# The opening of a two-layer trunk in another order: weight unit behind two rows, first projection by steps, forget-gate sum in the third

## The chip, the cores and the metric

The kernel runs on one core of a Trainium2 chip. The metric is device microseconds (us) for one execution. All times of the trace are counted from the start of the profiled span.

## The reference, cut to what matters

The trunk has two layers on 512 tokens of 1024 channels. Layer 0 mixes tokens by forgetting attention with 16 heads of 64 channels; layer 1 by a gated recurrence. After each mixer follow a layer norm, a gated ConvFFN (2816 wide), a second layer norm and a gated embedding. The change touches the start of layer 0 alone:

```python
proj = x @ w_in
q, k, v, fg = jnp.split(proj, [D_MODEL, 2 * D_MODEL, 3 * D_MODEL], axis=-1)
log_f = jax.nn.log_sigmoid((fg + b_f).astype(jnp.float32))
c = jnp.cumsum(log_f, axis=1).transpose(0, 2, 1)
logits = jnp.einsum("bhqd,bhkd->bhqk", q_i, k).astype(jnp.float32) * scale
logits = logits + c_i[..., None] - c[:, :, None, :]
probs = jax.nn.softmax(logits, axis=-1)
```

## The kernel before, in words

**Storage.** Activations lie channels first: eight tiles of 128 channels by 512 tokens (`x[:, m, :]`, "rows" below). Every float32 product is made of three products of a high and a low part (`three`, L402): high by high (L404), weight high by input low (L405), weight low by input high (L406). ScalarE (ACT) makes the high part of an input row (L1186), VectorE (DVE) the low part (L913). Weights come in units of 512 KB, eight 128x128 blocks, which the SP queue loads into one of four stage slots (L333) and GpSimd (POOL) splits, one instruction for the high part (L386) and four for the low part (L390), after a tiny instruction (L384) that waits for the load and for the last user of the slot.

**Order of the opening.** Each engine's order is written out by hand; semaphores join them.

- SP issues the loads of rows 0 to 3 (L303, two rows each), then weight units (L333). ACT issues the forget gate's weights `wf` and bias `bf` (L1178, L1179), rows 4 to 7 (L1181) and the column constants (L1182).
- TensorE (PE) first multiplies all eight rows by the forget weights, plain float32 of two passes a row (L447), once both `wf` and `bf` are there. Then it waits for all eight low parts (L556) and makes the projections of head pair 0: q to bank 0, k to bank 1, v to bank 0 (`project`, L472, over `whole_tile`, L408, 24 matmuls each). Between the eight steps of a projection other work is hung in (`beside`): the transposes of the forget gate (`turn_forget`, L455) in the first; the cumulative sum (`sum_forget`, L463) and blocks 0 to 2 of the turn of x to tokens (`first_block`, L440) in the second; the turn of columns (`turn_columns`, L553) and blocks 3 to 7 in the third. `sum_forget` waits for DVE's log-sigmoid steps (L921 to L928, some 16 small instructions, with one exponential on ACT, L1190).
- DVE then prepares the lambda of the recurrence (L934, L936), reads the queries (L944 to L953), copies the cumulated rows (L995, L997), makes the low part of the keys (`keys_low`, L960), and finishes the lambda chain (`log1p_twice`, L840 to L853, L1003 to L1007) before the first softmax maxima (L968).
- ACT copies the first three turned blocks (L1176), stores the cumulated rows to DRAM (L1194), waits for that store, loads a pair's rows back and reads the keys out of bank 1 (`keys`, L1205 and L1210), then copies `flat` (L1265) and the other five blocks, and the values (L1218).
- The first scores (L485 to L489) wait for the turned blocks, queries, low keys and rows. From there a loop over head pairs interleaves the projections of pair j with scores, turned probabilities (L505) and value sums (L517) of pair j - 1.

Of the kernel before, what the change touches and what calls it, by code (L numbers as in the profile page):

```python
# [21 lines left out]
P = 128  # L22
SEQ = 512
D_MODEL = 1024
DEPTH = 2
# [8 lines left out]
KT = D_MODEL // P  # L34
# [98 lines left out]
def hybrid_trunk_kernel(nc, xT, pT, w_square, w_down, w_forget, b_forget, w_lru, columns, outT):  # L133
    phases = plan()
    with ExitStack() as ctx:
        def sem(name):
            return ctx.enter_context(nc.semaphore(name))
# [18 lines left out]
        x = place("x", [P, KT, SEQ], F32)  # L156
# [22 lines left out]
        a = [tmp_at]  # L179
# [4 lines left out]
        a = [shared]  # L184
# [48 lines left out]
        unit_split = sem("unit_split")  # L233
        unit_used = sem("unit_used")
        x_loaded = [sem(f"x_loaded{n}") for n in range(KT // 2)]
        fg_w_loaded, cols_loaded = sem("fg_w_loaded"), sem("cols_loaded")
        consts_set = sem("consts_set")
        x_hi_ready, x_lo_ready = sem("x_hi_ready"), sem("x_lo_ready")
        mix_hi_ready, mix_lo_ready = sem("mix_hi_ready"), sem("mix_lo_ready")
# [59 lines left out]

        @block.sync  # L300
        def _(sp):
            for n in range(KT // 4):
                sp.dma_start(x[:, 2 * n:2 * n + 2, :], xT[:, 2 * n:2 * n + 2, :]).then_inc(x_loaded[n], 16)  # L303
            def norm_rows(n):
                if n == 0:
                    sp.wait_ge(flat_stored, 16)
                else:
                    sp.wait_ge(norm_ready, n * 2 * QT)
                src = rows_dram[n // 2, (n % 2) * 16:(n % 2) * 16 + 16, :].rearrange("a n -> (a n)")
                sp.dma_start(rows[:].rearrange("p a n -> p (a n)"),  # L310
                             src.partition_broadcast(P)).then_inc(rows_loaded, 16)

            square_first = 0
            for name, ph in phases.items():
                base, n, layer = square_first, len(ph.slots), int(name[-1]) if name[-1] in "01" else 0
                for i in rounds(sp, ph):
                    for r, place_at in enumerate(ph.slots):
                        s = place_at % SLOTS
                        sp.wait_ge(unit_split, ph.stage_free(i, r))
                        to = stage[:, s, :]  # L320
                        if name.startswith("down") or name.startswith("out"):
                            half, kp = r // (n // 2), r % (n // 2)
                            w, u = (w_down, layer * KT + half * 4) if name.startswith("down") else \
                                (w_square, base + half * 4)
                            src = w[u:u + 4, :, kp * 2 * P:(kp + 1) * 2 * P].rearrange("a p n -> p a n")
                            to = to.rearrange("p (a n) -> p a n", a=4)
                        elif name in ("rgx", "rgg"):
                            src = w_square[base + (r // 2) * 4 + r % 2 + (2 if name == "rgg" else 0)]
                        elif ph.iters == 1:
                            src = w_square[base + r]  # L330
                        else:
                            src = w_square[bass.ds(i * n + (base + r), 1), :, :].rearrange("a p n -> (a p) n")
                        sp.dma_start(to, src).then_inc(unit_loaded[s], 16)  # L333
                if name == "qkv":
                    norm_rows(0)
                if name.startswith("up"):
                    norm_rows(2 * layer + 1)
                if name == "gate0":
                    norm_rows(2)
                    sp.wait_ge(unit_used, phases["down0"].done(0, FT - 1))  # L340
                    sp.dma_start(w_ai[:], w_lru.rearrange("m p n -> p m n")).then_inc(lru_w_loaded, 16)
                if name == "rgg":
                    square_first += 2 * n
                elif name != "rgx" and not name.startswith("down"):
                    square_first += ph.iters * n

            for m in range(KT):
                sp.wait_ge(emb_added, KT + m + 1)
                sp.dma_start(outT[m], x[:, m, :]).then_inc(stored, 16)
            sp.wait_ge(stored, 16 * KT)  # L350
# [45 lines left out]
        def _(pe):  # L396
# [43 lines left out]
                    mm = pe.transpose(banks[bank][:, t * P:(t + 1) * P], x[:, m, t * P:(t + 1) * P], ident[:])  # L440
                mm.then_inc(block_turned, 1)

            pe.wait_ge(fg_w_loaded, 32)
            for k in range(KT):
                if k % 2 == 0:
                    pe.wait_ge(x_loaded[k // 2], 16)
                mm = pe.matmul(banks[5][0:HEADS, :], wf[:, k, :], x[:, k, :], start=(k == 0), stop=(k == KT - 1))  # L447
            mm.then_inc(fg_done, 1)

            def turn_forget():  # L450

# [20 lines left out]
            def project(j, r, bank, beside={}):  # L472
                whole_tile(qkv, j, r, bank, in_hi, in_lo, beside)
# [67 lines left out]
            def first_block(m):  # L541

                if m >= 3:
                    pe.wait_ge(x_tok_ready, m - 2)
                turn_block(m, 2 + m % 3)

            def turn_columns():
# [3 lines left out]
                for layer in range(DEPTH):  # L551
# [1 line left out]
                    mm = pe.transpose(banks[6][0:32, P + layer * P:2 * P + layer * P], cols[:, c:c + 32], ident[:])  # L553
                mm.then_inc(flat_done, 1)

            pe.wait_ge(x_lo_ready, KT)  # L556
            project(0, 0, 0, {1: turn_forget})
            project(0, 1, 1, {3: sum_forget, 4: lambda: first_block(0), 5: lambda: first_block(1),
                              6: lambda: first_block(2)})
            pe.wait_ge(q_read, 1)  # L560
            project(0, 2, 0, {1: turn_columns, 2: lambda: first_block(3), 3: lambda: first_block(4),
                              4: lambda: first_block(5), 5: lambda: first_block(6), 6: lambda: first_block(7)})
            pe.wait_ge(x_tok_ready, KT)
            pe.wait_ge(flat_read, 1)
            with pe.Fori(1, PAIRS) as j:
# [271 lines left out]
        def _(dve):  # L837
# [76 lines left out]
                                  ALU.subtract).then_inc(x_lo_ready, 1)  # L914


            dve.wait_ge(fg_done, 1)
            dve.tensor_scalar(z_chan[:], banks[5][0:HEADS, :], bf[:, 0:1], None, ALU.add).then_inc(fg_chan, 1)
            z, e, r0, r1, acc, minus_log = (fg[:, n, :] for n in range(6))
# [240 lines left out]
        def _(act):  # L1160
# [13 lines left out]
            def token_block(m, bank):  # L1174
                act.wait_ge(block_turned, m + 1)
                act.copy(x[:, m % KT, :], banks[bank][:]).then_inc(x_tok_ready, 1)  # L1176

            act.dma_start(wf[:], w_forget).then_inc(fg_w_loaded, 16)  # L1178
            act.dma_start(bf[:], b_forget).then_inc(fg_w_loaded, 16)  # L1179
            for n in range(KT // 4, KT // 2):  # L1180
                act.dma_start(x[:, 2 * n:2 * n + 2, :], xT[:, 2 * n:2 * n + 2, :]).then_inc(x_loaded[n], 16)  # L1181
            act.dma_start(cols[:], columns).then_inc(cols_loaded, 16)  # L1182
# [5 lines left out]

            act.wait_ge(fg_abs, 1)
            act.activation(fg[:, 1, :], fg[:, 1, :], ACT.Exp, scale=-1.0).then_inc(fg_exp, 1)  # L1190
            for m in range(3):
                token_block(m, 2 + m % 3)
            act.wait_ge(fg_rows, 1)
            act.dma_start(c_dram, c_rows[:].bitcast(F32)).then_inc(fg_stored, 16)  # L1194
# [19 lines left out]
            def values(j, turned):  # L1214
                act.wait_ge(unit_used, phases["qkv"].done(j, 2))
                if turned:
                    act.wait_ge(vt_done, j)
                act.copy(v_chan[:], banks[0][:]).then_inc(kv_read, 1)  # L1218

            def token_values(j):  # L1220
                act.wait_ge(vt_done, j + 1)
# [39 lines left out]
            act.sem_inc(pt_read, 1)  # L1261
            act.sem_inc(exp_ready, 1)
            keys(0, False)
            act.wait_ge(flat_done, 1)
            act.copy(flat[:].rearrange("p a n -> p (a n)"), banks[6][0:32, P:P + DEPTH * P]).then_inc(flat_read, 1)  # L1265
            for m in range(3, KT):
                token_block(m, 2 + m % 3)
            act.wait_ge(flat_read, 1)
            act.dma_start(rows_dram.rearrange("l r n -> r l n"), flat[:]).then_inc(flat_stored, 16)
            values(0, False)  # L1270
# [222 lines left out]
```

## Time and profile before

| what | value |
|---|---|
| median of 3 runs | 1329.36 us (1327.84 to 1331.38) |
| the profiled execution | 1330.12 us |
| its span | 1328.4 us |
| PE busy | 1297.2 us, 98% |
| granted TensorE clock, mean | 0.993 |
| POOL, DVE, ACT busy | 858.2, 539.0, 407.7 us |
| HBM traffic | 117.83 MB read, 2.20 MB written |

The profiled execution is 0.76 us longer than the median. Its span covers first to last instruction; 1.7 us lie around it. A timeline row gives start, duration, engine, line, operation, tiles and, in brackets, the idle time before it with what ended it. PE starts are exact, but matmul durations overlap the next one; start-to-start distances are used. A granted clock of 1.00 is the 2.4 GHz level, 0.50 the 1.2 GHz level.

### The profile page before, as it was taken

To read this page: it belongs to the slowest core of one execution; us is meant where nothing else is said; L and a number is where in the kernel's file an instruction comes from. 1 tells how busy PE (TensorE), PEld (TensorE's weight loads), DVE (VectorE), ACT (ScalarE), POOL (GpSimd) and SP (SyncE) were. 2 spreads that over 40 slices of the span, in tenths; PEclk is the share of its full clock that TensorE was granted. 3 is DMA by queue.
4 is the path that set the end of the run, shared out by engine and by line. 5 is a ranking of instruction groups with operands and counts; after the bars stand their busy time and mean duration, and the time that the engine had idled before them with its cause. 6 is when DMAs were issued, how large, how long until landed. Compare 5 with 4: busy or idle time off the path is not lost.

```text
span 1328.4 us, 17615 instructions
## 1 busy us (share of the span) xinstructions
PE 1297.2 (98%) x5758; PEld 1018.8 (77%) x5758; DVE 539.0 (41%) x826; ACT 407.7 (31%) x678; POOL 858.2 (65%) x1166
## 2 busy tenths in 40 slices
PE   6999999998999999999999999998999999999998
PEld 3766666676888888888888767877888888888886
DVE  6533344445444444411073357173444444301252
ACT  1443343411433333300033367112333333300041
POOL 6343445524978787777767645737877778777563
PEclk9999999998999999999999999998999999999999
DMA  5111113211232223333324222312322233333221
GB/s 183 52 48 63 48 51 108 80 47 64 96 107 97 95 95 126 95 111 95 99 90 161 79 80 64 109 47 83 111 95 95 97 99 130 111 101 95 80 88 55
DMA packets 57146, 120.58 MB, mean 91 GB/s; under 512 B 3744, under 2 KB 35808, under 8 KB 56592
## 3 DMA queue, kind: packets, MB, share of 16 engines
q1 hardware_dynamic: 56048, 117.45, 27.0%
q10 hardware_dynamic: 1056, 2.58, 0.6%
q8 instruction: 25, 0.41, 0.1%
q14 instruction: 17, 0.14, 0.0%
HBM read 117.83 MB, written 2.20 MB: 90 GB/s over the span
## 4 chain that ended last, share of the span: by engine, by line
PE 81%; issue 6%; ACT 3%; POOL 3%; DVE 2%; POOLq 2%; ACTq 1%; DMA 1%; DVEq 0%; SPq 0%
PE bank L404 17%; PE bank L406 16%; PE bank L405 16%; PE bank L424 6%; PE bank L423 6%; PE bank L425 6%; PE bank L517 3%; PE bank L655 2%; PE bank L656 2%; PE bank L660 2%; POOLq L387 2%; ACT probs L1232 1%; POOL w_lo L390 1%; POOL far_lo L390 1%; POOLq L385 1%
## 5 line engine op out<-in xcount | busy, mean ns | idle before, releaser
L390 POOL TENSOR_TENSOR w_lo<-stage,w_hi 128x256 fp32r<-128x256 f32 x800 | 589.5, 767 | 29.4 <-issue 0.3
L386 POOL TENSOR_SCALAR w_hi<-stage 128x1024 fp32r<-128x1024 f32 x200 | 210.5, 1053 | 179.1 <-PE bank L425 74.6
L404 PE MATMUL bank<-x_hi,w_hi 128*128 128x512 f32 x704 | 274.4, 390 | 0.0
L406 PE MATMUL bank<-x_hi,w_lo 128*128 128x512 f32 x704 | 274.0, 389 | 0.0
L405 PE MATMUL bank<-x_lo,w_hi 128*128 128x512 f32 x704 | 274.0, 389 | 0.0
L384 POOL TENSOR_TENSOR waiter<-waiter 128x1 f32<-128x1 f32 x112 | 24.8, 221 | 238.2 <-PE bank L406 161.5
L406 PEld LDWEIGHTS bank<-x_hi,w_lo 128*128 128x128 f32 x704 | 132.2, 188 | 27.4
L405 PEld LDWEIGHTS bank<-x_lo,w_hi 128*128 128x128 f32 x704 | 132.2, 188 | 27.3
L404 PEld LDWEIGHTS bank<-x_hi,w_hi 128*128 128x128 f32 x704 | 132.2, 188 | 27.3
L1034 DVE SCALAR_TENSOR_TENSOR tmp<-bank,cols,tmp 128x511 f32<-128x511 f32 x88 | 65.9, 749 | 207.7 <-ACT tmp L1288 196.7
L404 PE MATMUL bank<-in_hi,w_hi 128*128 128x512 f32 x320 | 138.7, 433 | 1.9 <-POOL w_lo L390 1.4
L424 PE MATMUL bank<-w_lo,h_hi 128*128 128x512 f32 x352 | 138.7, 394 | 0.0
L423 PE MATMUL bank<-w_hi,h_hi 128*128 128x512 f32 x352 | 138.4, 393 | 0.0
L425 PE MATMUL bank<-w_hi,h_lo 128*128 128x512 f32 x352 | 136.7, 388 | 0.0
L405 PE MATMUL bank<-in_lo,w_hi 128*128 128x512 f32 x320 | 126.6, 396 | 0.0
L406 PE MATMUL bank<-in_hi,w_lo 128*128 128x512 f32 x320 | 126.4, 395 | 0.0
L863 DVE SCALAR_TENSOR_TENSOR bank<-x,bank 128x512 f32<-128x512 f32 x32 | 22.2, 693 | 204.3 <-PE bank L425 203.4
L1288 ACT ACTIVATE tmp<-bank,cols 128x512 f32<-128x512 f32 x88 | 63.8, 776 | 60.0 <-PE bank L406 59.7
L404 PEld LDWEIGHTS bank<-in_hi,w_hi 128*128 128x128 f32 x320 | 60.5, 189 | 25.7 <-issue 16.0
L423 PEld LDWEIGHTS bank<-w_hi,h_hi 128*128 128x128 f32 x352 | 66.1, 188 | 15.2
L425 PEld LDWEIGHTS bank<-w_hi,h_lo 128*128 128x128 f32 x352 | 66.1, 188 | 14.8
L424 PEld LDWEIGHTS bank<-w_lo,h_hi 128*128 128x128 f32 x352 | 66.2, 188 | 13.0
(166 smaller groups left out, 1763.1 us busy)
## 6 DMA issues: line engine op xcount, KB each, us to landing
stage<-w_square SPq DMA_DIRECT2D x164, 512.0 KB, 3.3
stage<-w_down SPq DMA_DIRECT2D x44, 512.0 KB, 3.7
rows<-norm_rows SPq DMA_DIRECT2D x4, 1024.0 KB, 5.6
outT<-x SPq DMA_DIRECT2D x8, 256.0 KB, 2.0
x<-xT SPq DMA_DIRECT2D x2, 512.0 KB, 5.1
x<-xT ACTq DMA_DIRECT2D x2, 512.0 KB, 8.4
p_in<-pT ACTq DMA_DIRECT2D x2, 512.0 KB, 3.3
w_ai<-w_lru SPq DMA_DIRECT2D x1, 1024.0 KB, 8.4
```

The costliest lines, as they stand in the source:

```text
L386: pool.tensor_scalar(high[:, s, :], stage[:, s, :], 1.0, 0.0, ALU.mult, ALU.add)
L387: pool.drain()
L390: piece = pool.tensor_tensor(low[:, s, to], stage[:, s, to], high[:, s, to].bitcast(F32), ALU.subtract)
L404: pe.matmul(out, w_hi[:, s, c:c + P], m_hi, start=first, stop=False)
L405: pe.matmul(out, w_hi[:, s, c:c + P], m_lo, start=False, stop=False)
L406: return pe.matmul(out, w_lo[:, s, c:c + P], m_hi, start=False, stop=last)
L423: pe.matmul(four(out), m_hi, wide_hi, start=first, stop=False)
L424: pe.matmul(four(out), m_hi, wide_lo, start=False, stop=False)
L425: return pe.matmul(four(out), m_lo, wide_hi, start=False, stop=last)
L517: mm = pe.matmul(banks[7][h * HEAD_DIM:(h + 1) * HEAD_DIM, kt * P:SEQ], v_tok[:, kt, h * HEAD_DIM:(h + 1) * HEAD_DIM], probs_t[:, c0:c0 + ...
L1034: dve.scalar_tensor_tensor(t[:, 1:SEQ], banks[r][:, 0:SEQ - 1], cols[:, bass.ds(c + 1, 1)], t[:, 1:SEQ], ALU.mult, ALU.add)
L1288: act.activation(tmp[:, r, :], banks[r][:], ACT.Identity, bias=cols[:, bass.ds(c + 3, 1)], scale=cols[:, bass.ds(c + 2, 1)]).then_inc(conv ...
```

## The change

SP loads only rows 0 and 1 and goes on to the weight units; rows 2 and 3 go to ACT's queue, behind `wf` and ahead of `bf`, and `bf` has a semaphore of its own that DVE waits for. PE multiplies rows 0 to 5 by the forget weights, waits for weight unit 0, and then runs the q projection step by step, each step waiting for its own low part alone; the forget products of rows 6 and 7 stand ahead of its steps 0 and 1, the forget transposes ahead of step 6. The k projection has four turned blocks, the v projection the forget sum (ahead of its step 1), the columns and four blocks, and it writes to bank 5, so that the wait for the queries' read goes. ACT copies `flat` and all eight turned blocks before it stores the cumulated rows and takes up the keys.

```diff
-            for n in range(KT // 4):
-                sp.dma_start(x[:, 2 * n:2 * n + 2, :], xT[:, 2 * n:2 * n + 2, :]).then_inc(x_loaded[n], 16)
+            sp.dma_start(x[:, 0:2, :], xT[:, 0:2, :]).then_inc(x_loaded[0], 16)
...
-            pe.wait_ge(fg_w_loaded, 32)
-            for k in range(KT):
+            def forget(k):
                 if k % 2 == 0:
                     pe.wait_ge(x_loaded[k // 2], 16)
                 mm = pe.matmul(banks[5][0:HEADS, :], wf[:, k, :], x[:, k, :], start=(k == 0), stop=(k == KT - 1))
-            mm.then_inc(fg_done, 1)
+                if k == KT - 1:
+                    mm.then_inc(fg_done, 1)
...
-            pe.wait_ge(x_lo_ready, KT)
-            project(0, 0, 0, {1: turn_forget})
-            project(0, 1, 1, {3: sum_forget, 4: lambda: first_block(0), 5: lambda: first_block(1),
-                              6: lambda: first_block(2)})
-            pe.wait_ge(q_read, 1)
-            project(0, 2, 0, {1: turn_columns, 2: lambda: first_block(3), 3: lambda: first_block(4),
-                              4: lambda: first_block(5), 5: lambda: first_block(6), 6: lambda: first_block(7)})
+            pe.wait_ge(fg_w_loaded, 16)
+            for k in range(KT - 2):
+                forget(k)
+            unit_ready(qkv, 0, 0)
+            for k in range(KT):
+                if k < 2:
+                    forget(KT - 2 + k)
+                pe.wait_ge(x_lo_ready, k + 1)
+                if k == KT - 2:
+                    turn_forget()
+                mm = three(banks[0][:], 0, k * P, in_hi[:, k, :], in_lo[:, k, :], k == 0, k == KT - 1)
+            mm.then_inc(unit_used, 1)
+            project(0, 1, 1, {1: lambda: first_block(0), 3: lambda: first_block(1), 5: lambda: first_block(2),
+                              6: lambda: first_block(3)})
+            project(0, 2, 5, {0: sum_forget, 1: turn_columns, 2: lambda: first_block(4), 3: lambda: first_block(5),
+                              4: lambda: first_block(6), 5: lambda: first_block(7)})
...
+            dve.wait_ge(fg_b_loaded, 16)
             dve.wait_ge(fg_done, 1)
...
             act.dma_start(wf[:], w_forget).then_inc(fg_w_loaded, 16)
-            act.dma_start(bf[:], b_forget).then_inc(fg_w_loaded, 16)
+            act.dma_start(x[:, 2:4, :], xT[:, 2:4, :]).then_inc(x_loaded[1], 16)
+            act.dma_start(bf[:], b_forget).then_inc(fg_b_loaded, 16)
...
-            for m in range(3):
+            for m in range(4):
+                token_block(m, 2 + m % 3)
+            act.wait_ge(flat_done, 1)
+            act.copy(flat[:].rearrange("p a n -> p (a n)"), banks[6][0:32, P:P + DEPTH * P]).then_inc(flat_read, 1)
+            for m in range(4, KT):
                 token_block(m, 2 + m % 3)
             act.wait_ge(fg_rows, 1)
...
-                act.copy(v_chan[:], banks[0][:]).then_inc(kv_read, 1)
+                act.copy(v_chan[:], banks[0 if turned else 5][:]).then_inc(kv_read, 1)
...
             keys(0, False)
-            act.wait_ge(flat_done, 1)
-            act.copy(flat[:].rearrange("p a n -> p (a n)"), banks[6][0:32, P:P + DEPTH * P]).then_inc(flat_read, 1)
-            for m in range(3, KT):
-                token_block(m, 2 + m % 3)
             act.wait_ge(flat_read, 1)
```

## Rows read from the trace of the kernel before

**Rows 1.** Chain that ended last, 0 to 62 us: start, us, what

```profile
35.94 1.93 DMA forget_rows<-c_rows
...
41.03 0.69 DVE k_b L960
...
49.41 0.70 DVE stat L968
```

**Rows 2.** Timeline of ACT: high parts of the rows, and what they waited for

```profile
5.51 1.14 ACT L1186 CAST in_hi<-x 128x512 fp32r<-128x512 f32 x2 [0.61 <-DMA x<-xT]
6.81 1.14 ACT L1186 CAST in_hi<-x 128x512 fp32r<-128x512 f32 x2 [0.15 <-DMA x<-xT]
9.07 1.14 ACT L1186 CAST in_hi<-x 128x512 fp32r<-128x512 f32 x2 [1.13 <-DMA x<-xT]
11.63 1.14 ACT L1186 CAST in_hi<-x 128x512 fp32r<-128x512 f32 x2 [1.42 <-DMA x<-xT]
```

**Rows 3.** DMA queues in 5 to 6 us: packets, MB, share (q1 SP, q10 ACT)

```profile
q1 hardware_dynamic: 88, 0.30, 74.5%
q10 hardware_dynamic: 39, 0.11, 27.7%
```

**Rows 4.** DMA queues in 9 to 10 us

```profile
DMA packets 106, 0.42 MB, mean 422 GB/s; under 512 B 3, under 2 KB 3, under 8 KB 106
```

**Rows 5.** Timeline of POOL: splits of units 0, 1 and 5

```profile
9.89 0.58 POOL L384 TENSOR_TENSOR waiter<-waiter 128x1 f32<-128x1 f32 x1 [5.71 <-DMA stage<-w_square]
...
17.24 2.81 POOL L390 TENSOR_TENSOR w_lo<-stage,w_hi 128x256 fp32r<-128x256 f32 x4
...
46.27 2.81 POOL L390 TENSOR_TENSOR w_lo<-stage,w_hi 128x256 fp32r<-128x256 f32 x4
```

**Rows 6.** The forget products (L447) alone in two stretches: PE busy (x instructions)

```profile
6.03:9.16 3.13, 3.13 (x4) 0.58 (x5) 1.00 1.02 408
9.16:14.47 5.31, 5.31 (x13) 1.07 (x11) 1.00 0.69 275
```

**Rows 7.** Timeline of PE

```profile
6.03 8.44 PE L447 MATMUL bank<-x,wf 128*16 128x512 f32 x16 [6.03 <-DMA bf<-b_forget]
15.88 0.47 PE L404 MATMUL bank<-in_hi,w_hi 128*128 128x512 f32 x1 [1.41 <-POOL w_lo L390]
...
22.11 0.39 PE L404 MATMUL bank<-in_hi,w_hi 128*128 128x512 f32 x1
...
28.34 3.47 PE L463 MATMUL bank<-up_to,fg 128*16 128x512 f32 x8 [3.28 <-DVE fg L928]
...
33.01 0.60 PE L440 MATMUL bank<-ident,x 128*128 128x128 f32 x4
...
34.16 0.60 PE L440 MATMUL bank<-ident,x 128*128 128x128 f32 x4
...
43.32 0.60 PE L440 MATMUL bank<-ident,x 128*128 128x128 f32 x4
...
45.00 0.49 PE L485 MATMUL bank<-k_a,q_a 66*128 66x512 f32 x1 [0.38 <-issue]
...
52.98 0.50 PE L485 MATMUL bank<-k_a,q_a 66*128 66x512 f32 x1
...
60.28 0.55 PE L505 MATMUL bank<-ident,probs 128*128 128x128 f32 x3 [1.03 <-ACT probs_t L1242]
```

**Rows 8.** Timeline of DVE

```profile
17.91 0.23 DVE L921 COPY fg<-bank 128x64 f32<-128x64 f32 x1 [2.65 <-PE bank L455]
...
47.10 0.62 DVE L853 SCALAR_TENSOR_TENSOR lam<-lam 128x8 f32<-128x8 f32 x1
```

**Rows 9.** Line 851 alone, 15 to 60 us: ns min/median/max, first and last start

```profile
L851 DVE SCALAR_TENSOR_TENSOR lam<-lam x7: 166/168/959, 44.2 to 46.5; 128x8 f32<-128x8 f32 x7
```

**Rows 10.** Stretches by clock: PE, PEld, DVE, ACT, POOL busy, PEclk, DMA share, GB/s

```profile
29.37:32.78 3.41, 3.41 (x10) 1.44 (x8) 3.19 (x5) 0.00 (x0) 0.00 (x0) 0.50 0.44 154
316.09:322.92 6.83, 5.63 (x17) 3.94 (x15) 1.48 (x3) 0.00 (x0) 6.47 (x10) 0.50 0.36 136
```

More of the change, by code:

```diff
@@ L235, in hybrid_trunk_kernel @@
         x_loaded = [sem(f"x_loaded{n}") for n in range(KT // 2)]
-        fg_w_loaded, cols_loaded = sem("fg_w_loaded"), sem("cols_loaded")
+        fg_w_loaded, fg_b_loaded, cols_loaded = sem("fg_w_loaded"), sem("fg_b_loaded"), sem("cols_loaded")
         consts_set = sem("consts_set")
```

## The prediction

> **What bounds the kernel now.** I read the page first: PE is busy 98% of the span, so a change of order can only win or lose where PE stands or runs slowly. PE's timeline shows where it stands in the opening: until 6.03 us, for `bf`; 1.41 us before 15.88, for the split of unit 0; 3.28 us before 28.34, for the forget steps; 0.38 us before 45.00; 1.03 us before 60.28, for ACT [rows 7]. The stretches by clock add one thing: after that stand of 3.28 us the granted clock is 0.50, the 1.2 GHz level, from 29.37 to 32.78 [rows 10]. But a PE gap only counts if the chain that ended last runs through it. That chain goes, in the opening, over unit 0, the forget steps, the forget sum (28.34), three turned blocks that follow, the store of the cumulated rows (35.94), the low keys (41.03), the lambda chain on DVE, the first maxima (49.41), and ACT's exponentials, and it comes back to PE at 60.28 [rows 1, 7]. PE itself is off it from 36 to 60 us. So two chains have to be carried through to 60.28: one over PE, one over ACT and DVE. From there on PE is nearly always busy, and a shift stays.
>
> **The parts, worked out.** The sum is made against the profiled execution.
>
> *Loads.* SP's queue brought rows 0, 1 at 5.51 and rows 2, 3 at 6.81, ACT's queue rows 4, 5 at 9.07 and rows 6, 7 at 11.63 [rows 2]; unit 0 came at about 9.8, when POOL began [rows 5]. Each is 0.52 MB. Now unit 0 stands where rows 2, 3 stood, so I take 6.8. Rows 2, 3 take the place of rows 4, 5 (9.1), rows 4, 5 that of rows 6, 7 (11.6), and rows 6, 7 come after. All queues together move 0.42 MB a us [rows 4]; 0.5 MB more, with SP's queue running dry midway, gives 13.2 (bounds: 1.3 us behind 11.6, the full rate, which is 12.9; 2.6 us, the half, 14.2). A load moved to ACT's queue thus comes 2.3 us later, because that queue had only 0.11 of 0.41 MB in 5 to 6 us [rows 3]. The Trainium skill, "DMA: Bandwidth & Descriptors", "Queues, rings and completion order", says that each DMA engine takes turns between the queues it has work for; were the shares even from the start, rows 2, 3 would be there by about 7.2 and rows 6, 7 by 12.0, PE would be free for unit 0 at 12.5, and the sum below would be 0.9 us better. The row decides here: the shares were uneven.
>
> *Forget products.* Without `bf` PE starts at 5.55, not 6.03. A pass costs 3.13/4 = 0.8 us at first and 0.43 later [rows 6]. Rows 0, 1: four passes, to 8.95. Rows 2, 3 from 9.1 to 10.8; rows 4, 5 from 11.6 to 13.35. Unit 0 is no wait: POOL starts at 6.9 and needs 5.9 at most (9.89 to 15.74), 4.3 at the pace of unit 1 (ready at 20.05) [rows 5], so it is split by 11.2 to 12.8. PE begins the q projection at 13.4, where it began at 15.88 [rows 7].
>
> *First projection.* 15.88 to 22.11 is 6.2 us [rows 7], with the forget transposes in it; the four forget passes moved in add 1.75. End: 21.35, against 22.11. That is only 0.75 earlier: the early start is mostly spent on the forget products that were there anyhow. The waits for single low parts are nothing: the last low part is there by about 15.5 (13.2, 1.14 for ACT's two [rows 2], then DVE's) and step 7 comes at 20.7. `bf`'s wait on DVE is for a load that lands before fg_done (about 16).
>
> *Second projection.* 24 matmuls are 5.6, a turned block adds 0.45 (33.01 to 34.16 is a block and three matmuls, 1.15 [rows 7]): 7.4, to 28.75. ACT copies these blocks as they come; it has nothing else.
>
> *Forget sum.* The transposes end at 19.9 now (17.9 before [rows 8]), two us later. The DVE steps took 17.9 to 28.3, 10.4 us, since most ran beside POOL's splits: with POOL busy a small DVE step costs 0.62 [rows 8], with POOL idle 0.17 [rows 9]. POOL's fourth split waits for PE's last use of unit 0 (21.35) and ends 4.3 later, at about 25.7, and seven steps of 0.3 behind it give 27.8; were they slow to the end, 30.3. PE comes to the sum at 28.75 + 0.7 = 29.45. I take no stand; the bound is 0.85. The sum, 3.47 us with the clock mostly at 0.50 [rows 7, 10], is 2.15 at 1.00 by the widths 512, 384, 256, 128. So the third projection has its step 1 at 31.6.
>
> *Third projection.* Three steps with the columns (0.15) and three blocks come before the eighth block: 4 x 0.7 + 0.7 + 0.15 + 3 x 0.45 = 5.0. The eighth block is turned at 36.6, against 43.32 [rows 7], and the projection ends at 38.45. With bank 5 there is no wait for the queries; it would have bound nothing here before either. The cumulated rows (DVE, two copies after the queries) are ready at about 33.9 and wait for ACT.
>
> *Keys.* Here the change gives back. ACT stores the cumulated rows behind the eighth block, not the third. From the start of the copy before the store (35.9) to the low keys (41.03) is 5.1 us [rows 1]. Copy at 36.6 + 0.65 = 37.25, low keys at 42.35, against 41.03: 1.3 later. They take 1.5, so the first scores start at 43.85, against 45.00 [rows 7]. PE has stood 5.4 us by then. A stand of 3.28 us was followed by 3.41 us at half clock, which cost 1.7; another stretch had 6.83 us, 3.4 [rows 10]. I take the nearer, 1.7; bounds 0 and 3.4.
>
> *The two chains to 60.28.* PE: 43.85, plus 7.85 to the second scores (45.00 to 52.98 less a short wait), plus 1.7, is 53.4, against 52.98; plus 6.1 to the transposes (7.3 less 1.03 of stand) is 59.5. DVE: low keys to maxima took 8.4 [rows 1]. Seven of its steps ran beside POOL's split that starts with the third projection's end (46.27 is its low part [rows 5]) at 0.6 or more. Now that split runs 38.6 to 43, before the lambda chain, so seven steps cost 0.24 instead of 0.6 on average: 4.23 becomes 1.7, the chain 5.8. Maxima at 48.15 (49.41 before), which does not bind PE. The second head's maxima follow PE's scores: 53.4 + 1.9, plus 4.2 to PE's need, is 59.5 again. So 59.5 against 60.28: **0.8 us saved**, 1329.3 for the profiled execution (1330.12), and as that lies 0.76 above the median, 1328.6 on the median's scale.
>
> **What a measurement can tell.** 0.3% is 4.0 us, so 1325.4 and 1333.4 are the borders. The working has no 4 us in either direction.
>
> **Rivals.**
> - *A, slower: keys behind the token copies, and a cold PE.* Place: ACT's queue before the store. If rows 6, 7 come at 14.2 (+1.0), the forget steps stay slow (+0.85), and the half clock lasts 6.83 us (3.4), PE is back at 59.5 + 1.0 + 0.85 + 1.7 = 63.05: 2.8 slower, 1332.2. It decides from an eighth block at 37.4 on (with 1.7 for the clock). Beyond 4 us it would need that block after 39.7. For it: the bounds above. Against: PE's work up to there is counted in rows. Chance 0.20, of which 0.09 is past 4.0.
> - *B: the lambda chain stays slow.* 8.4 us put the maxima at 50.75, the second scores at 54.3, and PE back at 60.4 to 61.4: about 0.1 to 1.1 slower, 1330. The row against it is the 0.17 [rows 9]. A rule speaks against it too: the Trainium skill, "SBUF — State Buffer", "Who interferes with whom", has VectorE instructions with two SBUF inputs and GpSimd ones that read SBUF block each other wholly; 0.17 and 0.62 for such steps agree. Chance 0.15.
> - *C, faster: the clock is spared.* No half clock after the stand: 57.8 against 60.28, 2.5 saved, 1326.9. If, besides, one of the later half-clock stretches such as 316.09 to 322.92 (3.4 us [rows 10]) fell away with the new timing, it would be 5.9, 1323.5. Chance 0.15, of which 0.08 is past 4.0.
> - *D: the order does nothing*, because the first projection still ends near 22. It does end at 21.35, but the forget stand of 3.28 us goes anyway, by its later place; if all that were lost again before 60.28, it would be 1329.4. Chance 0.05.
> - The forecast itself: 0.45.
>
> **The numbers.** Predicted 1328.6. The range takes C without the later stretch and A up to its price, with 1 us for the runs' own spread: 1325.2 to 1332.8. Faster by over 0.3% has 0.08, slower 0.09, within 0.83.
>
> **What would show it.** Right: q projection near 13.4; no PE stand at 25 to 28; forget sum in some 2.2 us; eighth block near 36.6; a PE stand of 5 us before scores at 43.9, then half clock; low keys near 42.4; lambda steps all near 0.17; third transposes (60.28) near 59.5. Wrong: rows 6, 7 later than 14.2, an ACT queue that takes up the keys later than 40, or a second stand of over 1 us between 44 and 60.

## The result and the profile after

The changed kernel takes 1332.3 us (median of 19 runs, 1330.66 to 1334.65) against 1330.1 us of the kernel before (19 runs beside them). The ratio is 1.0020, with a 95% interval of 1.0014 to 1.0027: slower by 2.7 us (the medians differ by 2.2), less than the 0.3% that was set as a border, but clear of the noise, and not the 0.8 us gain of the forecast. The forecast of 1328.6 was counted from the median of three runs, 1329.36.

The profiled execution spans 1331.8 us, 3.4 more than before. It took 1333.66 us, 1.4 above the median, while the profile of the kernel before lies on its median. Eight of the 19 executions had a mean granted clock of 0.990, as the profiled one, and ten had 0.992. The marks below thus show one of the slower executions, with a stretch of half clock that others probably lack; run a3 shows what that is worth. In what follows a "stand" is a time in which PE waits between two instructions, and "half clock" a granted clock of 0.50.

The chain that ended last, kernel after, 0 to 66 us (start, us, what), is the place to begin:

```profile
1.56 7.06 DMA stage<-w_square
...
13.43 1.18 POOL w_lo L389
14.65 1.03 PE bank L446 x2
...
17.24 1.82 PE bank L446 x2
...
40.29 0.45 PE bank L439 x4
40.77 1.94 DMA forget_rows<-c_rows
...
45.86 0.68 DVE k_b L970
...
47.53 0.79 PE bank L485
...
59.85 0.70 DVE stat L978
...
63.77 0.59 ACT probs_t L1257
64.40 0.55 PE bank L505 x3
```

It runs over unit 0, then over PE up to the eighth turned block, and from there over ACT's store of the cumulated rows (L1209) and the low keys to the first scores. The lambda chain, which stood in it before [rows 1], is gone from it. In its place stands PE itself, from 47.53 on.

PE's timeline, kernel after, has the same marks as [rows 7]:

```profile
5.66 6.89 PE L446 MATMUL bank<-x,wf 128*16 128x512 f32 x12 [5.66 <-DMA wf<-w_forget]
14.65 1.03 PE L446 MATMUL bank<-x,wf 128*16 128x512 f32 x2 [2.11 <-POOL w_lo L389]
...
24.56 0.40 PE L403 MATMUL bank<-in_hi,w_hi 128*128 128x512 f32 x1
...
32.71 2.33 PE L463 MATMUL bank<-up_to,fg 128*16 128x512 f32 x8
...
40.13 0.60 PE L439 MATMUL bank<-ident,x 128*128 128x128 f32 x4
...
47.53 0.79 PE L485 MATMUL bank<-k_a,q_a 66*128 66x512 f32 x1 [5.40 <-DVEq L972]
...
57.98 0.39 PE L485 MATMUL bank<-k_a,q_a 66*128 66x512 f32 x1
...
64.40 0.55 PE L505 MATMUL bank<-ident,probs 128*128 128x128 f32 x3 [0.27 <-ACT probs_t L1257]
```

| mark on PE | before | forecast | after |
|---|---|---|---|
| first projection begins | 15.88 | 13.4 | 14.65 |
| second projection begins | 22.11 | 21.35 | 24.56 |
| forget sum | 28.34 | 29.45 | 32.71 |
| eighth block turned | 43.32 | 36.6 | 40.13 |
| first scores | 45.00 | 43.85 | 47.53 |
| second scores | 52.98 | 53.4 | 57.98 |
| third transposes of the first head ("the return") | 60.28 | 59.5 | 64.40 |

The return is the mark by which the experiments are compared below; in the changed kernel it is 4.1 us late. The span is only 3.4 us longer, for 0.7 came back later: PE's last stand of the layer norm is 0.87 us where it was 1.20, and one near 790 us is 0.67 where it was 1.06.

Two stretches of the changed kernel are at half clock (columns as in [rows 10]):

```profile
15.67:19.08 3.41, 3.41 (x7) 0.97 (x6) 0.00 (x0) 0.00 (x0) 3.26 (x5) 0.50 0.44 154
46.39:53.22 6.83, 5.69 (x18) 4.29 (x19) 5.12 (x22) 1.25 (x3) 0.13 (x1) 0.50 0.23 83
```

The first follows a stand of 2.11 us, the second begins in one of 5.40. The kernel before had one stretch of 3.41 us, after 3.28 us of stand.

ACT's and POOL's timelines, kernel after, show when rows and unit 0 came and how long the split took:

```profile
5.71 2.18 ACT L1197 CAST in_hi<-x 128x512 fp32r<-128x512 f32 x4
10.10 1.14 ACT L1197 CAST in_hi<-x 128x512 fp32r<-128x512 f32 x2 [2.21 <-DMA x<-xT]
12.68 1.14 ACT L1197 CAST in_hi<-x 128x512 fp32r<-128x512 f32 x2 [1.43 <-DMA x<-xT]
```

```profile
8.87 0.19 POOL L383 TENSOR_TENSOR waiter<-waiter 128x1 f32<-128x1 f32 x1 [4.70 <-DMA stage<-w_square]
...
10.44 4.17 POOL L389 TENSOR_TENSOR w_lo<-stage,w_hi 128x256 fp32r<-128x256 f32 x4
14.56 0.64 POOL L383 TENSOR_TENSOR waiter<-waiter 128x1 f32<-128x1 f32 x1
```

Rows 2 and 3 were there by 6.8 (ACT goes through four rows without a wait), rows 4 and 5 at 10.1, rows 6 and 7 at 12.7: all earlier than forecast. Unit 0 came at 8.7, later than forecast, and its low part took 4.17 us where unit 1's took 2.81 [rows 5]. Unit 0 was slow before the change too (POOL timeline, kernel before):

```profile
12.07 3.67 POOL L390 TENSOR_TENSOR w_lo<-stage,w_hi 128x256 fp32r<-128x256 f32 x4
```

### The profile page after: what moved, and what is told of

It is laid out like the page before. It is cut to its first block, busy times and chain, and to the rows that moved or that the text cites. A ratio compares the mean times of both kernels' runs of the same rounds, so it can differ in the third digit from the quotient of the medians.

```text
span 1331.8 us, 17615 instructions
## 1 busy us (share of the span) xinstructions
PE 1300.0 (98%) x5758; PEld 1019.8 (77%) x5758; DVE 532.3 (40%) x826; ACT 407.9 (31%) x678; POOL 858.5 (64%) x1166
## 4 chain that ended last, share of the span: by engine, by line
PE 83%; issue 5%; ACT 3%; POOL 3%; POOLq 2%; DVE 1%; ACTq 1%; DMA 1%; DVEq 0%; SPq 0%
PE bank L403 17%; PE bank L405 17%; PE bank L404 17%; PE bank L423 6%; PE bank L422 6%; PE bank L424 6%; PE bank L517 3%; PE bank L664 2%; PE bank L665 2%; PE bank L669 2%; POOLq L386 1%; ACT probs L1247 1%; POOL w_lo L389 1%; POOL far_lo L389 1%; PE bank L485 1%
```

## The experiments

Each kernel is compared with runs of the kernel before on the same chip. "Return" is the mark of the table above, from one profiled execution (60.28 before, 64.40 after). The ratios rest on 10 to 12 executions of each kernel, b7's on 5 and c1's on 6, and for the change itself on 19.

| run | ratio to before | 95% interval | first scores | return |
|---|---|---|---|---|
| the change | 1.0020 | 1.0014 to 1.0027 | 47.53 | 64.40 |
| a1 first part alone | 1.0018 | 1.0008 to 1.0027 | 46.93 | 62.53 |
| a2 second part alone | 1.0012 | 1.0003 to 1.0021 | 45.31 | 62.12 |
| a3 early keys | 1.0013 | 1.0004 to 1.0022 | 44.38 | 61.78 |
| a4 products before scores | 1.0004 | 0.9995 to 1.0013 | 47.56 | 62.36 |
| b5 forget products ahead | 1.0005 | 0.9996 to 1.0014 | 45.07 | 62.15 |
| b6 products at both stands | 0.9997 | 0.9988 to 1.0006 | 46.60 | 61.40 |
| b7 all mended | 0.9963 | 0.9949 to 0.9976 | 42.82 | 58.67 |
| b8 loads back | 1.0022 | 1.0013 to 1.0032 | 48.94 | 65.39 |
| c1 mended, 18 products | 0.9970 | 0.9958 to 0.9982 | 43.03 | 57.33 |
| c2 mended, none | 0.9992 | 0.9983 to 1.0001 | 42.75 | 59.44 |
| c3 before, lambda moved | 0.9987 | 0.9979 to 0.9996 | 45.03 | 59.02 |
| c4 mended, loads back | 0.9975 | 0.9967 to 0.9984 | 43.61 | 57.60 |

**a1: the first part alone.** Loads, forget products and first projection as changed; the rest, ACT's order and v's bank included, as before.

```diff
-            project(0, 1, 1, {1: lambda: first_block(0), 3: lambda: first_block(1), 5: lambda: first_block(2),
-                              6: lambda: first_block(3)})
-            project(0, 2, 5, {0: sum_forget, 1: turn_columns, 2: lambda: first_block(4), ...
+            project(0, 1, 1, {3: sum_forget, 4: lambda: first_block(0), 5: lambda: first_block(1),
+                              6: lambda: first_block(2)})
+            pe.wait_ge(q_read, 1)
+            project(0, 2, 0, {1: turn_columns, 2: lambda: first_block(3), ...
```

> The kernel before with the first part alone: the loads, the forget products and the first projection by steps as changed; second and third projections, banks and ACT's order as before. Theory 1 (in the changed kernel a late unit 0 and the half-clock stretch behind PE's 2.1 us stand push the end of the first projection from 22.1 to 24.5, and the way of the keys adds the rest): the forget steps end near 31, the forget sum starts 2.7 us later than before, everything up to the transposes at 60.28 shifts by it, 1332.8 or 2.7 us slower than before. Theory 2 (the first part is neutral, ACT's late keys alone cost the time): within 0.7 us of before.

The time is near the expected 2.7 us (2.4 by the ratio) and speaks against theory 2, but it does not come by the expected steps. PE timeline of a1, and a row of its stretches by clock:

```profile
14.15 1.03 PE L446 MATMUL bank<-x,wf 128*16 128x512 f32 x2 [0.81 <-POOL w_lo L389]
...
29.56 4.45 PE L463 MATMUL bank<-up_to,fg 128*16 128x512 f32 x8 [4.10 <-DVE fg L939]
```

```profile
27.53:34.36 6.83, 4.80 (x9) 1.43 (x10) 5.58 (x14) 0.00 (x0) 0.42 (x1) 0.50 0.24 77
```

Here the stand before the unit was 0.81 us and no half clock followed, and still the forget sum is 1.2 us late and takes 4.45 us instead of 3.47. The first part, with its forget transposes ahead of step 6, feeds DVE's forget steps later; in the old second projection that makes a stand of 4.10 us where there were 3.28, and 6.83 us of half clock around it where there were 3.41. The scores are 1.9 us late and the return 2.25.

**a2: the second part alone.** Projections 2 and 3, bank 5 and ACT's order as changed; loads and first projection as before.

```diff
-            project(0, 1, 1, {3: sum_forget, 4: lambda: first_block(0), ...
-            pe.wait_ge(q_read, 1)
-            project(0, 2, 0, {1: turn_columns, 2: lambda: first_block(3), ...
+            project(0, 1, 1, {1: lambda: first_block(0), 3: lambda: first_block(1), ...
+            project(0, 2, 5, {0: sum_forget, 1: turn_columns, 2: lambda: first_block(4), ...
```

> The kernel before with the rest of the change alone: forget sum in the third projection with its own bank, four turned blocks in the second, ACT's keys behind all turned blocks; loads, forget products and first projection as before. Theory 1 (both parts cost, each by a clock stretch): eighth block turned at 37.4, low keys at 43.1, first scores at 44.7, a half-clock stretch behind the stand, PE back at the transposes at 60.5 to 62.2 instead of 60.28: 0.2 to 1.9 us slower than before. Theory 2 (late keys alone are the cause): as slow as the whole change, 2.2 us or more.

Theory 1 holds. The scores start after the same stand of 5.40 us as in the changed kernel, with 6.82 us of half clock around them; a row of stretches and one of PE's timeline of a2:

```profile
44.73:51.55 6.82, 6.24 (x19) 4.74 (x20) 4.73 (x21) 1.24 (x3) 0.00 (x0) 0.50 0.23 78
```

```profile
45.31 0.79 PE L485 MATMUL bank<-k_a,q_a 66*128 66x512 f32 x1 [5.40 <-DVEq L961]
```

The return is 1.84 us late. The two losses add up to 4.09, against 4.12 for the whole change, but that is luck: a1 loses by a stand before the forget sum, which the whole change does not have, and the whole change by half clock before 20 us, which a1 does not have. Each part does cost something without the other. Theory 2 of this run, 2.2 us or more, is unlikely by the return; the ratio alone (0.4 to 2.8 us) does not exclude it.

**a3: keys behind the fifth block.**

```diff
-            for m in range(4, KT):
-                token_block(m, 2 + m % 3)
+            token_block(4, 2 + 4 % 3)
             act.wait_ge(fg_rows, 1)
...
             keys(0, False)
+            for m in range(5, KT):
+                token_block(m, 2 + m % 3)
```

> The changed kernel, but ACT stores the cumulated rows and reads the keys behind the fifth turned block, and copies blocks 5 to 7 after them. Theory 1 (the late keys make a 5.4 us stand and with it 6.8 us of half clock): store at 37.4 instead of 40.8, low keys at 42.5, first scores at 44.2, stand 2.1 us, half clock 3.4 us at most, PE back near 60 instead of 64.4: 3.5 to 4.5 us faster than the changed kernel, 1329 to 1330, level with before. Theory 3 (the loss comes from the first part, the keys are hidden): within 1 us of the changed kernel.

The keys came as expected (low keys at 42.3, scores at 44.38). Still the stand was 3.75 us, not 2.1, and the half clock lasted the full 6.83 us:

```profile
44.53:51.36 6.83, 6.83 (x21) 5.05 (x22) 4.33 (x19) 2.06 (x7) 0.50 (x1) 0.50 0.23 78
```

Part of this is not the keys' doing. Up to the fourth turned block the program is that of the changed kernel, and yet its opening ran otherwise, as the PE timeline of a3 shows:

```profile
5.71 7.63 PE L446 MATMUL bank<-x,wf 128*16 128x512 f32 x12 [5.71 <-DMA wf<-w_forget]
14.70 1.03 PE L446 MATMUL bank<-x,wf 128*16 128x512 f32 x2 [1.35 <-POOL w_lo L389]
...
31.21 2.33 PE L463 MATMUL bank<-up_to,fg 128*16 128x512 f32 x8
```

PE needed 7.63 us for the twelve forget products, not 6.89, and so stood 1.35 us for unit 0, not 2.11. No half clock followed, and the forget sum came at 31.21 instead of 32.71. PE was then ready for the scores 1.5 us earlier, which is why its stand there was long; the wait for ACT's copies of blocks 5 to 7 adds only some 0.4 us. The scores gained 3.15 us and the return 2.6, but 1.5 us of either is the missing half clock, and the early keys are worth about 1.65 us of the scores and 1.1 of the return. In time, 1.0013 against 1.0020 is no more than a hint, and theory 3 (within 1 us) fits it too. The 3.5 to 4.5 us of the expectation did not come.

**a4: unused products before the scores.**

```diff
             pe.wait_ge(flat_read, 1)
+            for n in range(24):
+                pe.matmul(banks[6][:], in_hi[:, 0, 0:P], in_hi[:, 0, :], start=True, stop=True)
```

> The changed kernel plus 24 products into a free bank between the third projection and the first scores, where PE stood 5.4 us; their results are not used. Theory 1 (half of the loss is the clock, not the stand): first scores still at 47.5, no half clock from 46.4 to 53.2, second scores at 55.2 (then bound by ACT's exponentials) instead of 58.0, PE back at 61.4 instead of 64.4: about 3 us faster than the changed kernel, 1329.4. Theory 4 (the chain over DVE and ACT holds the time whatever PE's clock): no change against the changed kernel.

This run has the same order, and its first scores stand at 47.56 (47.53 in the changed kernel). Only the clock differs:

```profile
42.20:47.50 5.30, 5.30 (x24) 4.13 (x22) 1.47 (x3) 2.92 (x5) 4.07 (x6) 1.00 0.03 8
47.50:53.20 5.70, 5.70 (x32) 4.48 (x32) 4.12 (x20) 0.76 (x2) 0.00 (x0) 1.00 0.27 93
```

32 matmuls start in 47.5 to 53.2 here. The second scores come at 55.43 instead of 57.98 (2.55 us), the return at 62.36, behind a stand of 0.78 us for ACT, 2.0 us earlier. The 3 us expected left that stand out. In this run the first half is as in the profile of the change (stand of 2.05 us, then 3.41 us of half clock), so the two can be set side by side, and the ratios are apart as well, 1.0004 against 1.0020. Theory 4 falls.

**b5: forget products of rows 6 and 7 ahead of the unit's wait.**

```diff
-            for k in range(KT - 2):
+            for k in range(KT):
                 forget(k)
             unit_ready(qkv, 0, 0)
             for k in range(KT):
-                if k < 2:
-                    forget(KT - 2 + k)
                 pe.wait_ge(x_lo_ready, k + 1)
```

> The changed kernel, but the forget products of rows 6 and 7 stand ahead of the wait for unit 0 (as rows 0 to 5 do), so they fill PE's 2.1 us stand. Theory 1 (the first part loses by that stand: 1.75 us of products are put behind the unit's arrival, and the clock falls): no half clock at 15.7 to 19.1, first projection ends at 20.9 instead of 24.5, forget sum at 29.0 to 29.4, first scores near 43.8, PE back at 60.4 to 60.8 instead of 64.4: 3.6 to 4 us faster than the changed kernel, 1328.5, level with before or up to 1.5 us under it. Theory 5 (unit 0's late arrival alone is the loss, the place of the products is nothing): within 1 us of the changed kernel.

The first part of this came out: no half clock before 44, the forget sum at 30.26 instead of 32.71 (with a stand of 0.90 us for DVE's steps, which ran beside POOL's splits for longer than I had counted), the scores at 45.07. But those scores still stand behind 5.40 us and 6.83 us of half clock, and the return is 62.15, 2.25 us earlier, not 3.6 to 4: the scores were already 1.3 us behind the expectation, by that stand and a later sum. Theory 5 gives less than 1 us. The return alone does not refute it: 1.5 us of the 2.25 is the half clock that a3 was spared with the products in their old place. The ratio, 1.0005 against 1.0020, is on theory 1's side, but the intervals touch, so the place of the products is likely a cause and not proven one.

**b6: products at both stands.** As a4, and eight more ahead of the wait for unit 0.

```diff
+            pe.wait_ge(x_lo_ready, 1)
+            for n in range(8):
+                pe.matmul(banks[6][:], in_hi[:, 0, 0:P], in_hi[:, 0, :], start=True, stop=True)
             unit_ready(qkv, 0, 0)
```

> The changed kernel plus 8 unused products while PE waits for unit 0, and 24 before the first scores. Order, stands and queues are as changed; only the clock differs. Theory 1: no half clock before 316; unit 0 still at 14.65, first projection ends at 22.7, first scores at 45.8, PE back at 60.6: 1.8 us faster than the same kernel with the later products alone (1330.6), so 1328.8; what the change costs beside the clock is then nothing or a small gain. Theory 2 (stands cost, not the clock): 1330.6 or more.

Theory 1: scores at 46.60, return at 61.40, no half clock before 317. Both marks are 0.8 us later than expected; 0.6 of it because the eight products ran past the unit's arrival and moved the start from 14.65 to 15.26. Against the change, the two stretches of half clock cost 3.0 us of return, and 1.0020 becomes 0.9997 with intervals apart. The order with a warm PE is level with the kernel before, which has a half clock of its own.

**b7: everything mended.** The edits of b5 and a3, 12 unused products, the forget transposes ahead of step 2, and the lambda chain moved, with its exponential (L1211) behind the copy of the columns.

```diff
-                if k == KT - 2:
+                if k == 2:
                     turn_forget()
...
-            keys_low(0)
-
             dve.wait_ge(lam_exp, 1)
             log1p_twice(l0, le, l1, l1, l2)
...
             dve.tensor_scalar(lz, lam4[:, 5, :], -2.0, None, ALU.mult).then_inc(lam_abs, 1)
+            keys_low(0)
```

> The changed kernel with every cause found taken out: forget products 6 and 7 ahead of unit 0's wait, forget transposes ahead of step 2, ACT's store and keys behind the fifth turned block, the lambda chain on DVE between the cumulated rows and the low keys (its exponential behind the copy of the columns), 12 unused products before the first scores. Theory 1: forget sum at 29, low keys at 38 to 39, first scores at 40 to 41, maxima bound by the scores, PE back at 54 to 55 instead of 60.28 in the kernel before: 5 to 6 us faster than before, 1324 to 1325. If one of the waits behind it binds (units, probabilities): 1326 to 1327.

0.9963, 0.9949 to 0.9976: about 4.9 us faster than before and clear of both kernels. The time is between the two expectations. The low keys came at 40.75, not at 38 to 39, and the scores at 42.82, some 2 us later than hoped. PE timeline of b7:

```profile
42.82 0.49 PE L485 MATMUL bank<-k_a,q_a 66*128 66x512 f32 x1 [1.19 <-ACT x L1186]
```

and its chain that ended last:

```profile
34.12 3.46 DMA forget_rows<-c_rows
```

The copies of three blocks behind the keys add 0.4 us (2.07 us from low keys to scores, 1.67 in the changed kernel). The larger part is the store of the cumulated rows, which took 3.46 us where it took 1.93 before the change and 1.94 after. In b7 it ran beside the load of a weight unit (0.52 MB on SP's queue in the same stretch); in the kernel before and in the changed one nothing else was loaded meanwhile. a3 has the same, with 3.32 us. Of b7's five executions the profiled one is the slowest, 1328.28 us.

**b8: loads back in the changed kernel.**

```diff
-            sp.dma_start(x[:, 0:2, :], xT[:, 0:2, :]).then_inc(x_loaded[0], 16)
+            for n in range(KT // 4):
+                sp.dma_start(x[:, 2 * n:2 * n + 2, :], xT[:, 2 * n:2 * n + 2, :]).then_inc(x_loaded[n], 16)
...
-            act.dma_start(x[:, 2:4, :], xT[:, 2:4, :]).then_inc(x_loaded[1], 16)
```

> The changed kernel, but rows 2 and 3 are loaded by SP ahead of the weight units, as before. Theory 1 (unit 0 early is worth about 1 us, its split is what PE waits for): unit 0 lands at 9.8 and is split at 15.7, PE stands over 3 us before it and the clock falls, the first projection ends 1 us later than in the changed kernel, 1333 or 1 us slower. Theory 6 (the rows' lateness is what costs): faster than the changed kernel by 0.5 us or more.

PE timeline of b8:

```profile
16.05 1.15 PE L447 MATMUL bank<-x,wf 128*16 128x512 f32 x2 [2.92 <-POOL w_lo L390]
```

Unit 0 is ready 1.4 us later, the return 1.0 us later (65.39), with the same two lengths of half clock as in the changed kernel. By these marks the early load is a gain, and theory 6 is unlikely; in time (1.0022 against 1.0020) the two can't be told apart.

**c1, c2: how much the unused products carry.** The mended kernel with 18 and with none unused ones.

```diff
-            for n in range(12):
+            for n in range(18):
                 pe.matmul(banks[6][:], in_hi[:, 0, 0:P], in_hi[:, 0, :], start=True, stop=True)
```

```diff
-            for n in range(12):
-                pe.matmul(banks[6][:], in_hi[:, 0, 0:P], in_hi[:, 0, :], start=True, stop=True)
```

> The mended kernel with 18 instead of 12 unused products before the first scores. Theory 1 (a stand before the scores still costs by the clock behind it): the stand of 1.2 us before the scores and the half clock from 44.8 to 48.2 go, PE back at 56.9 instead of 58.7, 1.7 us faster than with 12: 1325.0. Theory 2 (only stands cost): as with 12, 1326.7.

> The mended kernel without any unused product. Theory 1: PE stands 3.9 us before the scores at 42.8, half clock of 3.4 or 6.8 us behind it, PE back at 58.7 to 60.4: 1326.7 to 1328.4, still under the kernel before. Theory 2 (only stands cost, and the scores start when their inputs are there): as with 12, 1326.7, for the scores start at the same time.

The first scores are at 43.03, 42.82 and 42.75 with 18, 12 and 0 products, the returns at 57.33, 58.67 and 59.44; the half clock before 100 us lasts 0, 3.41 and 6.83 us. That is theory 1 in the marks. Without products the mended order is level with the kernel before, 0.9992; with 18 it is 0.9970, with the intervals just apart (0.9983 and 0.9982 are their near ends). Between 12 and 18 the ratios don't tell (0.9963 against 0.9970). PE timeline of c2, a stand of 3.96 us:

```profile
42.75 0.79 PE L485 MATMUL bank<-k_a,q_a 66*128 66x512 f32 x1 [3.96 <-ACT x L1184]
```

**c3: one move in the kernel before.** The lambda chain goes ahead of the low keys, as in b7.

```diff
-            keys_low(0)
-
             dve.wait_ge(lam_exp, 1)
             log1p_twice(l0, le, l1, l1, l2)
...
+            keys_low(0)
...
+            act.wait_ge(lam_abs, 1)
+            act.activation(lam4[:, 1, :], lam4[:, 1, :], ACT.Exp, scale=-1.0).then_inc(lam_exp, 1)
             for m in range(3):
                 token_block(m, 2 + m % 3)
```

> The kernel before with one move: the lambda chain on DVE between the cumulated rows and the low keys, its exponential on ACT ahead of the first turned block. Theory 7 (before the change the maxima wait for the lambda chain, slowed by POOL's split; this is the path to PE at 60.28): maxima bound by the first scores, at 47.0 instead of 49.4; second scores 0.1 earlier; PE back at 59.1 instead of 60.28: 1.1 us faster than before, 1329. Theory 8 (PE is the only path that counts): no difference.

Theory 7, nearly to the number: DVE timeline of c3, where the first maxima wait for PE's scores and no longer for the lambda chain.

```profile
47.02 1.68 DVE L968 TENSOR_REDUCE stat<-bank 128x1 f32<-128x512 f32 x4 [4.49 <-PE bank L489]
```

Return at 59.02; 0.9987, 0.9979 to 0.9996. A single move of some 15 tiny instructions is worth 1.3 to 1.7 us in the old order.

**c4: loads back in the mended kernel.** b8's edit on b7.

```diff
-            sp.dma_start(x[:, 0:2, :], xT[:, 0:2, :]).then_inc(x_loaded[0], 16)
+            for n in range(KT // 4):
+                sp.dma_start(x[:, 2 * n:2 * n + 2, :], xT[:, 2 * n:2 * n + 2, :]).then_inc(x_loaded[n], 16)
```

> The mended kernel (12 unused products) with rows 2 and 3 loaded by SP ahead of the weight units, as before the change. Theory 1 (unit 0's early load is the one part of the first half that pays): unit 0 split at 15.7 instead of 14.6, PE's stand before it 1.3 us, no half clock there, all later by 1.1 us: 1327.8. Theory 6 (the load order is worth nothing once the forget products fill the wait): 1326.7.

The scores come at 43.61, 0.8 us later than in b7 (1.1 expected), yet the return is 57.60, earlier than b7's 58.67. PE timeline of c4:

```profile
43.61 0.50 PE L486 MATMUL bank<-k_a,q_a 66*128 66x512 f32 x1 [1.18 <-ACT x L1187]
```

The stand is 1.18 us, b7's 1.19 us, and b7 has 3.42 us of half clock from 44.77 on where c4 has none. Set beside c1, which has no half clock either, c4's return is 0.3 us later. So the load order is worth some tenths of a us here; the ratio, 0.9975 beside 0.9970, can't resolve it. The time, 1326.65 us, is what this run's theory 6 expected (1326.7), not theory 1's 1327.8: once the forget products fill the wait, the early load hardly pays.

## Why the prediction was wrong

**The loads: both assumptions off.** I let rows 2 and 3 come at 9.1 as rows 4 and 5 had; they came by 6.8. The Trainium skill, "DMA: Bandwidth & Descriptors", "Queues, rings and completion order", has each DMA engine take turns between the queues with work. The 7.2 us that I had worked out from it by even shares, and set aside, was the better guide there; but that sum, too, left unit 0 at 6.8. DMA rows of 3 to 5 us (packets, MB, share), kernel before:

```profile
q1 hardware_dynamic: 149, 0.55, 79.6%
q10 hardware_dynamic: 143, 0.05, 10.2%
```

and kernel after:

```profile
q1 hardware_dynamic: 89, 0.31, 48.3%
q10 hardware_dynamic: 173, 0.30, 40.5%
```

Before, ACT's queue had about as many packets as SP's (143 and 149) but a tenth of the bytes: it had only small pieces to move there, `wf` and `bf`. With rows behind `wf` it moved as much as SP's, whose bytes fell from 0.55 to 0.31 MB, and unit 0 came at 8.7 and not at 6.8.

**"Unit 0 is no wait": the step that failed.** The prediction put this wait at nothing, with the split done by 11.2 to 12.8; it was done at 14.6. The load explains it: unit 0 came 1.9 us after the 6.8 on which both bounds stood. The split itself took 5.7 us, inside the bound of 5.9: its low part took 4.17 us instead of unit 1's 2.81, while DVE made the low parts of rows 4 to 7 from 10.75 to 15.15, and the slow split of unit 0 before the change, from which the bound came, had that in it. PE, done with six rows at 12.55, stood for 2.11 us, and the two forget products moved behind the wait were then paid in full: four passes and the projection ran partly at half clock. The second projection began at 24.56 instead of 21.35. Of these 3.2 us, 1.25 are the later start and 1.7 the clock (half of 3.41). The late start is in every trace that has this first projection behind the unit's wait (14.15 in a1, 14.65 to 14.70 in the change, a3 and a4); the clock's part is not, as a3 shows. b5 shows it from the other side: with the products ahead of the wait there is neither stand nor half clock, and the sum comes 2.45 us earlier than in the change and 0.95 earlier than in a3.

**Second and third projection, forget sum.** Right in size: 24.56 to 32.71 is 8.15 us (8.1 forecast), the sum 2.33 us (2.15), the eighth block 7.4 us behind its start (7.15). There was no stand before the sum.

**Keys.** Right: 5.73 us from block to low keys (5.75 forecast), and the stand before the scores was 5.40 us (5.4). ACT stored the rows at 40.8, past the 40 that the prediction had named as a sign of being wrong. The delay before the scores was 1.67, not 1.5.

**The clock behind the stand.** This term was mis-sized, within its bounds: 1.7 taken, 3.4 the upper one. The stretch was 6.83 us long and cost 2.55 us by a4 (57.98 against 55.43). In a2, a3, b5 and c2, with stands of 3.75 to 5.40 us there, it was as long. The kernel before's 3.41 us behind 3.28 was the nearest row by length of stand, but not a fair price.

**The lambda chain.** Right: seven steps took 1.62 us, all at 0.17 (DVE timeline, kernel after), and the maxima were at 51.70.

```profile
49.04 1.62 DVE L860 SCALAR_TENSOR_TENSOR lam<-lam 128x8 f32<-128x8 f32 x7
...
51.70 1.68 DVE L978 TENSOR_REDUCE stat<-bank 128x1 f32<-128x512 f32 x4
```

Rival B falls with it; c3 shows that this chain was indeed what bound the maxima before.

**In sum.** 59.5 was forecast for the return and 64.40 came: 3.2 from the first projection, 0.5 on the way to the scores, 0.9 from the second half clock, 0.3 behind it. Of that last term 0.2 is a slip in the working (7.3 less 1.03 is 6.27, not 6.1). Another changes nothing: four passes of 0.8 us from 5.55 end at 8.75, not at 8.95, and rows 2 and 3 were awaited at 9.1. Rival A, ACT's late keys and a cold PE, named the mechanism of the second half and gave 1332.2, close to the measured 1332.3. That closeness is luck: it came to its sum by a later load of rows 6 and 7 and by a wait for slow forget steps, neither of which occurred, and not by the wait for unit 0.

## What to carry to other kernels

When work that could fill an engine's wait is moved behind that wait, price the wait at its worst case and not at its best: here a planned start 2.5 us earlier, with 1.75 us of products moved behind a unit that was late, became an end 2.45 us later, 1.7 of it by half clock. A queue's share read in one stretch says little of its share with other transfers on it; ask first whether it had anything large to move, and what a transfer moved to it takes from the others. A small transfer on the critical path is priced with what runs beside it: the same 64 KB store took 1.94 us alone and 3.46 beside a weight unit. Two profiles of equal code can differ by 1.5 us, so see that the part left alone ran alike before a gain is put down to the edit. A stand on TensorE has to be costed with the clock behind it, and independent work put into the stand, even unused products, can be worth more than a shorter chain; look as well for tiny instructions on a chain that could run while their engine idles.

## What was not expected of the hardware

Every half-clock stretch ahead of the last matmul in these traces is about 3.41 or 6.83 us long, with very different stands before it: 3.28 us (before), 2.11 us (after) and 2.92 us (b8) gave 3.41, and 3.75 to 5.40 us (a1, a2, a3, b5, c2 and the change) gave 6.83. The length of the stand alone does not decide: 1.19 us in b7 was followed by half clock and 1.18 us in c4 and 1.41 us in the kernel before were not; 2.05 us in a4 was, 1.35 us in a3 was not. Nor does the length of the stand give that of the stretch everywhere: near 316 us, stands of 2.91 and 0.68 us preceded 6.83 us in the kernel before and in the changed one. What decides between such cases stays open.

PE's first forget products ran slowly at a granted clock of 1.00: the passes began 0.83 to 0.86 us apart and later 0.43. The pace doubled near 9 us in the traces of the kernel before, the change and a4, and 1 to 2 us later in the other eleven. In the changed order that bears on how long PE stands for unit 0: 2.11 and 2.05 us in the change and a4, 1.35 and 0.81 in a3 and a1, and only the first two have half clock there.

A split on POOL that took 2.81 us alone took 4.17 us beside DVE's low parts, and DVE steps of 0.17 us took 0.6 beside POOL's: each slows the other. The kernel before had shown the first direction already, with 3.67 us for unit 0.
